# A hybrid decoder step on one core: heads rotated ahead of their inverse roots, negated maxima as biases, value chunks dealt out anew and added by DMAs

## What is computed

```python
def _layer(x, pe, pos, g_mix, w_in, g_v, w_s, b_s, g_q, g_k, w_oa, w_ob, w_o,
           g_ffn, w_ff1, w_ff2, g_ple, w_ple_gate, w_ple_proj, mix_a, mix_b):
    z = _rmsnorm(x, g_mix) @ w_in
    u, va, q, k, v, gate_a, gate_b = jnp.split(z, cuts, axis=-1)
    u = jax.nn.gelu(u)
    va = _rmsnorm(jax.nn.gelu(va), g_v)
    a = mix_a(u, va, w_s, b_s)
    q = _rotary(_rmsnorm(q.reshape(*lead, N_HEADS_B, HEAD_DIM), g_q), pos)
    k = _rotary(_rmsnorm(k.reshape(*lead, N_HEADS_B, HEAD_DIM), g_k), pos)
    b, kv_states = mix_b(q, k, v)
    merged = jax.nn.sigmoid(gate_a) * (a @ w_oa) + jax.nn.sigmoid(gate_b) * (b @ w_ob)
    x = x + merged @ w_o
    x = x + jnp.square(jax.nn.relu(_rmsnorm(x, g_ffn) @ w_ff1)) @ w_ff2
    gate = jax.nn.sigmoid(_rmsnorm(x, g_ple) @ w_ple_gate)
    x = x + gate * (pe @ w_ple_proj)
```

## Time and profile before

| | us |
|---|---|
| median of three runs | 1136.82 (1135.38 to 1138.96) |
| the profiled execution | 1137.38 |
| its span in the trace | 1136.0 |
| busy in it: PE, DVE, ACT, POOL | 1060.5, 719.9, 430.3, 229.7 |

### The profile page before, as it was taken

How to read it: one execution, slowest core, us unless ns; L and a number is a source line. 1 busy time by engine, 2 the same in 40 slices (tenths; PEclk the granted TensorE clock), 3 DMA queues, 4 the chain that set the end, 5 groups by cost and what they waited for, 6 DMA issues and landing times.

```text
span 1136.0 us, 21037 instructions
## 1 busy us (share of the span) xinstructions
PE 1060.5 (93%) x8448; PEld 1043.8 (92%) x8448; DVE 719.9 (63%) x995; ACT 430.3 (38%) x737; POOL 229.7 (20%) x367
## 2 busy tenths in 40 slices
PE   5989889998998989897999999999999999999996
PEld 5989879898888989887999999999999999999996
DVE  5669988888789866998947335443444444444552
ACT  5242355445533645424236443411421332233331
POOL 2331112102230001369800111100101101002300
PEclk9999989999999889899899999999999999999999
DMA  6645736676467743458763224564564555554412
GB/s 189 205 131 196 229 124 193 196 230 205 151 228 250 208 141 121 124 172 222 221 217 113 88 92 158 175 203 167 193 198 160 197 190 172 192 189 158 168 64 79
DMA packets 131007, 196.17 MB, mean 173 GB/s; under 512 B 31984, under 2 KB 108240, under 8 KB 129136
## 3 DMA queue, kind: packets, MB, share of 16 engines
q1 hardware_dynamic: 106448, 123.54, 34.0%
q0 software_dynamic: 10112, 63.08, 17.1%
q10 hardware_dynamic: 14368, 8.46, 2.5%
HBM read 186.07 MB, written 62.00 MB: 218 GB/s over the span
## 4 chain that ended last, share of the span: by engine, by line
PE 54%; DVE 23%; POOL 8%; issue 6%; ACT 4%; DMA 3%; SPq 1%; ACTq 0%; DVEq 0%; POOLq 0%
PE gm L1046 48%; POOL kv L1797 6%; DVE w_lo L1315 4%; DVE kv L1436 3%; DVE kv L1477 2%; DVE fin L1356 2%; DVE sq L1335 2%; ACT w_hi L617 2%; DVE acc L1483 2%; POOL st L1767 1%; DVE st L1327 1%; SPq L508 1%; DMA out_kvp<-fin 1%; PE gm L1022 1%; DVE rot L1365 1%
## 5 line engine op out<-in xcount | busy, mean ns | idle before, releaser
L1046 PE MATMUL gm<-h_hi,w_hi 128*128 128x272 f32 x1088 | 231.0, 294 | 11.2 <-DVE z L1379 4.9
L1046 PE MATMUL gm<-h_hi,w_lo 128*128 128x272 f32 x1088 | 227.8, 291 | 0.0
L1046 PE MATMUL gm<-h_lo,w_hi 128*128 128x272 f32 x1088 | 226.9, 290 | 0.0
L1315 DVE TENSOR_TENSOR w_lo<-w_raw,w_hi 128x1024 fp32r<-128x1024 f32 x150 | 178.0, 1227 | 75.2 <-ACT w_hi L617 73.4
L617 ACT CAST w_hi<-w_raw 128x1024 fp32r<-128x1024 f32 x150 | 150.1, 1047 | 152.1 <-PE gm L1046 116.5
L1022 PE MATMUL gm<-w_hi,h_hi 128*128 128x256 f32 x640 | 190.0, 297 | 4.4 <-DVE w_lo L1315 2.3
L1046 PEld LDWEIGHTS gm<-h_hi,w_hi 128*128 128x128 f32 x1088 | 173.1, 191 | 13.0 <-issue 11.1
L1023 PE MATMUL gm<-w_hi,h_lo 128*128 128x256 f32 x640 | 183.8, 287 | 0.0
L1024 PE MATMUL gm<-w_lo,h_hi 128*128 128x256 f32 x640 | 182.9, 286 | 0.0
L1046 PEld LDWEIGHTS gm<-h_lo,w_hi 128*128 128x128 f32 x1088 | 173.4, 191 | 0.0
L1046 PEld LDWEIGHTS gm<-h_hi,w_lo 128*128 128x128 f32 x1088 | 172.5, 192 | 0.0
(11 more groups left out here) (254 smaller groups left out, 1463.4 us busy)
## 6 DMA issues: line engine op xcount, KB each, us to landing
w_raw<-in_w_ff SPq DMA_DIRECT2D x64, 512.0 KB, 5.2
out_kvs<-in_cache_kv_w POOLq DMA_DIRECT2D x64, 510.0 KB, 4.2
w_raw<-in_w_in SPq DMA_DIRECT2D x60, 512.0 KB, 5.5
kv<-in_cache_kv_w SPq DMA_DIRECT2D x128, 128.0 KB
kv<-in_cache_kv_w SPq DMA_DIRECT2D x64, 256.0 KB
out_kvs<-in_cache_kv_w POOLq DMA_DIRECT2D x32, 508.0 KB, 4.7
kv<-in_cache_kv_w POOLq DMA_DIRECT2D x128, 64.0 KB, 3.5
w_raw<-in_w_o SPq DMA_DIRECT2D x8, 512.0 KB, 4.8
```

What stands on the lines that cost most here:

```text
L1046: last = nc.tensor.matmul(gm[:, 2 * b2 + half, 0:HALF], w, x[:, k0 + k, half * HALF:(half + 1) * HALF], start=first, stop=end)
L1315: vec.tensor_tensor(w_lo[:, r, cols], w_raw[:, hh], w_hi[:, r, cols].bitcast(F32), ALU.subtract).then_inc(w_lo_done, 1)
```

## The change

1. **Chunks.** `CHUNKS_AT` is given by a string, one digit a slot. Group 0's keys now start in slot 11 (before 9), its values run in slots 26 to 38 (before 24 to 37), with 11 of them in slots 30 to 35. Group 1's values run in slots 54 to 71 (before 72), 16 of 17 by slot 64. Group 2 has its keys in 72 to 79, its values in 80 to 84.
2. **Adds by DMA.** A value chunk of groups 0 and 1 after the first is only multiplied by DVE; POOL then issues a DMA that adds `kv` to `acc` (`add_values`, `accum_op=ALU.add`), in the slot after, once the add before it has landed. Who reuses the ring place or reads `acc` waits for `values_added` (`wait_values`).
3. **Heads.** DVE applies gain and rotation to the unscaled `z` in the unit's own slot (`rotate_heads`) and scales by the inverse root last (`scale_heads`), for sub 0 and 1 in the same slot behind the maxima, for sub 2 in the next. The two half products of the rotation become one. The factor 1/8 is put into the q gain by POOL once.
4. **Maxima.** `tensor_reduce` writes the negated maximum, which is ACT's bias; `ngm` goes. Both pieces of a pair are taken in its even slot, by DVE and by ACT.
5. **ACT's order.** Squares of sample rows, the tanh of gelu and the exponentials of the chunk weights move to the start of the next slot. DMAs of v sample rows go from ACT to POOL. The factor of gelu moves into the square, and DVE's two instructions for its inner part become one.
6. **Head of the program.** `gx_b` is issued ahead of `ident`; PE runs 22 matmuls on `ones` before its first transposes and 8 behind them.

```diff
+CHUNKS_IN_SLOT = ("000000000002203112002102012102212213002103003002112111"
+                  "103113122110000001131100121213200000000000")
+CHUNKS_AT = {_s: int(_n) for _s, _n in enumerate(CHUNKS_IN_SLOT)}
...
-        if s in S_AT:
+        if s in S_AT and not (paired(S_AT[s]) and S_AT[s] % 2):
             jobs.append(("piece", S_AT[s]))
+            if paired(S_AT[s]):
+                jobs.append(("piece", S_AT[s] + 1))
...
+        def added_by_dma(n):
+
+            return CHUNKS[n][0] == "values" and CHUNKS[n][1] < 2 and n != CH_FIRST["values", 0]
...
+        def wait_values(engine, n):
+
+            if added_by_dma(n):
+                engine.wait_ge(values_added, 16 * added_count(n))
+            else:
+                engine.wait_ge(values_used, sum(c[0] == "values" and not added_by_dma(x) for x, c in enumerate(CHUNKS[:n + 1])))
...
@@ ACT @@
-                    nc.scalar.activation(sq[0:NS, r, 0:256], z[0:NS, r, 0:256], ACT.Square).then_inc(sq_ready, 1)
...
+                if s >= 1 and UNITS[s - 1][4] == 2 and UNITS[s - 1][1] in ("k", "q", "va"):
+                    square_samples(s - 1)
+                if s >= 1 and UNITS[s - 1][1] in ("va", "u"):
+                    gelu_tanh_of(s - 1)
...
-                        e = nc.scalar.activation(prob[:, j % 2, w * x:w * x + w], s_bank(j)[:, w * x:w * x + w], ACT.Exp, scale=SCALE,
-                                                 bias=ngm[:, j % 2, x:x + 1])
+                        e = nc.scalar.activation(prob[:, j % 2, w * x:w * x + w], s_bank(j)[:, w * x:w * x + w], ACT.Exp,
+                                                 bias=O[:, x if g_ else 2 * pair + x, hd, 65:66])
...
@@ PE @@
+            pe.wait_ge(zeroed, 1)
+            busy(22)
             pe.wait_ge(ident_in, 16)
             x_transposes(0)
             x_transposes(1)
+            busy(8)
...
@@ DVE, rotate_heads @@
                     if fin_count(n - 2):
                         dve.wait_ge(fin_stored[n % 2], fin_count(n - 2))
...
+                vec.tensor_tensor(f.rearrange("p (h d) -> p h d", d=HD), z[0:rows, r, 0:256 * nt].rearrange("p (h d) -> p h d", d=HD),
+                                  bc(gain, 1, 4 * nt), ALU.mult).then_inc(z_used, 1)
...
+            def scale_heads(u):
+                rows, nt = shape_kq(u)
+                n = kqn(u)
+                dve.wait_ge(rstd_ready, n + 1)
+                f = fin[0:rows, n % 2, 0:256 * nt].rearrange("p (h d) -> p h d", d=HD)
+                vec.tensor_tensor(f, f, bc(st[0:rows, 1, 16 + 8 * (n % 2):16 + 8 * (n % 2) + 4 * nt], 2, HD), ALU.mult).then_inc(fin_ready, 1)
...
-                link(vec.tensor_reduce(m, sv, AX.X, ALU.max))
-                vec.tensor_scalar(ngm[:, j % 2, 0:512 // w], m, -SCALE, None, ALU.mult).then_inc(max_ready, 1)
+                vec.tensor_reduce(m, sv, AX.X, ALU.max, negate=True).then_inc(max_ready, 1)
...
                 if first:
                     out.then_inc(values_used, 1)
+                elif added_by_dma(n):
+                    out.then_inc(values_scaled, 1)
...
@@ POOL @@
+            gp.tensor_scalar(gq_b[:], gq_b[:], SCALE, None, ALU.mult).then_inc(gain_scaled, 1)
...
+            def add_values(n):
+
+                nk = CHUNKS[n][3]
+                pool.wait_ge(values_scaled, added_count(n))
+                if added_count(n) > 1:
+                    pool.wait_ge(values_added, 16 * (added_count(n) - 1))
+                else:
+                    pool.wait_ge(values_used, 1)
+                pool.dma_start(acc[:, 0:nk], kv[:, n % RING, 0:nk], accum_op=ALU.add).then_inc(values_added, 16)
...
+                for n in CH_AT.get(s - 1, []):
+                    if added_by_dma(n):
+                        add_values(n)
```

More of the change, by code:

```diff
@@ L652, in evacuate @@
                     r = stage_slot(u)
-                    nc.scalar.activation(two(sq[:, r]), src, ACT.Square).then_inc(sq_ready, 1)
+                    nc.scalar.activation(two(sq[:, r]), src, ACT.Square, scale=GELU_A ** 0.5).then_inc(sq_ready, 1)
                     nc.scalar.copy(two(z[:, r]), src).then_inc(unit_out, 1)
@@ L704, in evacuate, with gelu_tanh_of, square_samples @@
                     square_x(m, m, zc(u))
+            def gelu_tanh_of(u):
+                _, kind, _, _, sub = UNITS[u]
+                act.wait_ge(gelu_arg, GELU.index(u) + 1)
+                r = (zc(u) - 1) % 2
+                rows, n = (128, NT) if kind == "u" else (128, 512) if sub < 2 else (NS, 256)
+                nc.scalar.activation(sq[0:rows, r, 0:n], sq[0:rows, r, 0:n], ACT.Tanh, scale=GELU_B).then_inc(gelu_tanh, 1)
+            def square_samples(u):
+                r = (zc(u) - 1) % 2
+                act.wait_ge(unit_out, u + 1)
+                nc.scalar.activation(sq[0:NS, r, 0:256], z[0:NS, r, 0:256], ACT.Square,
+                                     scale=GELU_A ** 0.5 if UNITS[u][1] == "va" else 1.0).then_inc(sq_ready, 1)
             def merged_hi(m):
@@ L837, in tile_hi @@
                                    x_bank(a, half).rearrange("p (k n) -> p k n", k=4)).then_inc(h_hi_done, 1)
+            act.dma_start(gx_b[:], t["g_mix"].partition_broadcast(128)).then_inc(gx_in, 16)
             act.dma_start(ident[:], t["c_ident"]).then_inc(ident_in, 16)
[L840 removed]
             square_tile(0)
@@ L918, in _ @@
                     act.wait_ge(al_arg, 1)
-                    nc.scalar.activation(al[:], al[:], ACT.Exp, scale=SCALE).then_inc(al_exp, 1)
+                    nc.scalar.activation(al[:], al[:], ACT.Exp).then_inc(al_exp, 1)
                 if s == 65:
@@ L1251, in y_transposes, with busy @@
                 nc.tensor.transpose(psO[0:NS, 0:128], xT[:, m, SEQ:NT], ident[:]).then_inc(t_ready, 1)
+            def busy(n):
+                for _ in range(n):
+                    nc.tensor.matmul(gm[:, 3, 0:128], ones[:], ones[:], start=True, stop=True)
+            pe.wait_ge(zeroed, 1)
+            busy(22)
             pe.wait_ge(ident_in, 16)
@@ L1388, in gelu_inner @@
                 dve.wait_ge(sq_ready, sq_count(u))
-                link(vec.tensor_scalar(sq[0:rows, r, 0:n], sq[0:rows, r, 0:n], GELU_A, 1.0, ALU.mult, ALU.add))
                 dve.wait_ge(unit_out, u + 1)
-                vec.tensor_tensor(sq[0:rows, r, 0:n], sq[0:rows, r, 0:n], z[0:rows, r, 0:n], ALU.mult).then_inc(gelu_arg, 1)
+                vec.scalar_tensor_tensor(out=sq[0:rows, r, 0:n], in0=sq[0:rows, r, 0:n], scalar=1.0, in1=z[0:rows, r, 0:n],
+                                         op0=ALU.add, op1=ALU.mult).then_inc(gelu_arg, 1)
             def gelu_outer(u):
@@ L1649, in _ @@
                 if kind in ("k", "q"):
-                    sum_squares(s)
-                if kind in ("va", "u"):
+                    if sub < 2:
+                        sum_squares(s)
+                    rotate_heads(s)
+                if kind == "u" or kind == "va" and sub < 2:
                     gelu_inner(s)
@@ L1695, in _ @@
                     take_scores(job)
+                if kind in ("k", "q") and sub < 2:
+                    scale_heads(s)
                 for g_ in range(NG):
@@ L1824, in _ @@
                 p, kind, g, i, sub = UNITS[s]
+                if s >= 1 and UNITS[s - 1][1] == "v" and UNITS[s - 1][4] == 2:
+                    _, _, vg, vi, _ = UNITS[s - 1]
+                    pool.wait_ge(unit_out, s)
+                    cols = slice(256 * vi, 256 * vi + 256)
+                    pool.dma_start(t[f"kvs{vg}"][:, 1, WIN[vg] - T:WIN[vg], cols],
+                                   vn[NS * vg:NS * vg + NS, cols]).then_inc(vn_stored[vg], 16)
                 if kind in ("k", "q"):
```

119 lines of the change are left out of this document (55 added, 64 removed).

## The result

| | before | after |
|---|---|---|
| median, us | 1137.82 (4 runs) | 1231.53 (1227.55 to 1236.01, 4 runs) |
| ratio | | 1.0827 (95%: 1.0800 to 1.0853) |
| the profiled execution, its span | 1137.38, 1136.0 | 1236.01, 1234.6 |

The forecast was 1100 us in a range from 1082 to 1138. The change is 94 us slower, beyond the rival that was given 1176.

The account below looks back on a forecast made before the run. PE, busy 1060.5 of 1136.0 us, was taken as the bound, to gain only by less waiting or a higher clock. Recovered 50 less 6 (stores) and 7 (adds) made 37; 1137.4 - 37 - 0.6 = 1100 us, range 1082 to 1138.

Parts of the forecast that it names:

- I take 5 with the issue: Value chunks of groups 0 and 1: one 512 KB DMA add takes 5 us including its issue.
- priced at 7 us: Cost of the DMA adds: 4 us in group 1's v units plus 3 us from 349 us on.
- The bounds of 3 and 11: Limits for one add: below 3 us (2.0 and a second 256 KB), above 11 us (5.5 twice).
- Rival 1: DMA adds become the bound at 9 us each, giving 1176 us; decides from 7.6 us an add; chance 0.12.
- Heads rotated first: Rotating in the unit's own slot makes `fin` earlier; PE's 9.8 us and DVE's 14.7 us of waits go.
- a gain of most of 25 us: q, k and v units, 26 to 349 us: three quarters of 33.0 us of idle and clock loss recovered.
- DVE's 14.7 us for inverse roots: DVE's waits for GpSimd's inverse roots, 14.7 us, were to go with heads rotated first.
- The 17: 349 to 446 us (value rows, gated inputs, scores of group 2): four fifths of 21.1 us recovered.
- The merge: 446 to 547 us (merge of branch A and of the attention): a quarter of 21.7 us recovered, 5 us.
- The stores, 6 us: DVE overwriting `fin` waits for k-unit stores: 12 k units at 0.5 us each, 6 us lost.
- rival 2: DVE waits 2 us per k unit for stores, or adds take about 6 us; 1118 us; chance 0.24.
- The head: Head of the program: added matmuls raise PE's clock for unit 0, 3 us won; they take 5.3 us of idle time.

Follow-up runs that it names:

- e1: The changed kernel with all value chunks added by VectorE again instead of by DMA; 1139.83 us, 1.0028 of the kernel before.
- e12: e11 with the chunk table of e8, which keeps chunks out of the slots of sample rows; 1106.79 us, 0.9713 of the kernel before.
- e2: e1 with the chunk table (`CHUNKS_AT`) of the kernel before; 1142.07 us, 1.0038 of the kernel before.
- e11: e1 with gain, rotation and scaling of a unit in the next slot, as in the kernel before; 1113.40 us, 0.9773 of the kernel before.
- e5: e1 with a pair's two maxima ahead of the gain product and rotation in q and k slots; 1134.52 us, 0.9968 of the kernel before.
- e8: e5 with a chunk table that keeps chunks out of the sample rows' slots from slot 24 to 53; 1121.20 us, 0.9842 of the kernel before.
- e10: The change with its 33 DMA adds as plain copies, so value chunks are not summed; 1194.26 us, 1.0488 of the kernel before.

## Why the prediction was wrong, point by point

**The price of an add, "I take 5 with the issue", is the step that failed most.** From start to start it is 8.0 us (220 to 268 us) and 8.6 (512 to 547 us, four adds), and 7.4 to landing; the adds by DMA, priced at 7 us, cost 92 against adds on VectorE. The value was taken "nearest to GpSimd's own copy" at 4.2, a row from DRAM to DRAM that waits for no other. An add on an idle chip does take 4.8. Loads and a cache copy beside it bring the landing from 4.5 to 6.2 us; the rest, up to 7.4, is not explained by any run. The Trainium skill (DMA: Bandwidth & Descriptors, Anatomy of one DMA) gives an estimate of 3.2 us for 512 KB: a copy alone lands in 2.8, an add alone in 4.5 and one in the layer in 7.4, so the trace does not agree for adds. The bounds of 3 and 11 held it, and they should have set the range: by the prediction's own rule the sign turns at 7.6.

**Rival 1 was the mechanism, and too cheap.** Its rule gives 1176 at 9 us; at 8 to 8.6 us the kernel took 1231. It hid 40 us in the ring and in slots without chunks, and priced no clock: in units 36 to 53 PE's own work took 12 us more than in e1 (117.0 against 105.2). Which part of the 92 us comes through the ring, through the late inverse roots and through the panels is not separated. The signs named for it (GpSimd over 100 us in its own DMAs, scaling behind GpSimd, chunks behind loads) are all in the list. Against it stood only the copy's row.

**"Heads rotated first" was taken for a gain of most of 25 us; in the unit's own slot rotation and scaling lose 26 against the next slot.** The prediction counted what `fin` wins by being early (PE's wait for it did fall, from 9.8 to 2.2 us in e1), not what stands behind the rotation. DVE's 14.7 us for inverse roots were to go with it; in e1 they are 27.1, because the scaling now follows in the same slot. The sentence on the stores named the queue (the join, both maxima, the chunks), but for the wait, not for the 1.6 us of work itself. By stretch, in us won (e1, and e12 with neither adds nor early slot, against the earlier trace rows):

| units | forecast won | e1 | e12 |
|---|---|---|---|
| head | 3 | 2.1 | 1.4 |
| 1 to 53, q, k, v | 25 | -15.1 | 18.2 |
| 54 to 64 | 17 | 4.4 | 3.6 |
| 65 to 80, the merge | 5 | 13.2 | 13.2 |
| 81 to 111 (before from 547.1 to 684.4 us) | 0 | -4.2 | -5.9 |

Ahead of unit 81 36 of the 50 us were reachable, by another order and another table than the change's. The 17 was too much; the stretch of `va` and of the scores of group 2, which are not paired, gives 4, and no run takes its waits apart. The merge was too little; e2, with the old table, wins 5.8 there, so the table makes 7.4 of the 13.2. Behind unit 80 the prediction expected nothing either way, and 5.9 us are lost in e12, all but 0.1 in units 81 to 95 (77.5 us wide against 71.7): the clock is 0.96 there in place of 1.00, and PE waits 2.9 us for `sm`, which it did not before. No run shows the cause.

**The stores, 6 us,** are of the right order: DVE waits 11.2 us for those of k heads in the change, but in 4 places and not in 12, and 5.7 us in 3 places for sample rows of q on their way to `q_rows`, which the prediction did not count. What this costs PE no run isolates, nor rival 2.

**Chunks.** That the table is a term of its own was missed. The slots of sample rows, whose units keep PE busy for 1.8 to 6.1 us in e1, now hold up to three key chunks, 7.2 us of DVE's work. Corrected, it gives 6.6 us (e11 to e12) and 13 (e5 to e8).

**The head.** The size was right by the traces: unit 0 ends at 23.9 us in place of 26.6, which is 2.7 for the 3. Its cover was thinner than thought: the matmuls on `ones` take 8.0 us, not 5.3, and end 0.1 us before the first transposes.

```profile
1.84 7.96 PE L1287 MATMUL gm<-ones 128*128 128x128 f32 x44 [1.84 <-POOL V L1819]
9.89 1.06 PE L1130 MATMUL psT<-ident,xn 128*128 128x128 f32 x8
```

**The range.** Its lower end is said to be 55 us won, with 3 for the adds, 3.5 at the head and nothing for stores. These terms give 50 + 0.5 - 3 = 47.5, an end at 1089 and not at 1082. It changes nothing here.

## What to carry to other kernels

A chain of DMAs in which each waits for the one before is an engine: price it from issue to issue under the load that stands beside it, times its length, before work is moved to it; here 1.3 us of VectorE was exchanged for 8 us of a queue. When an operation moves to an earlier place in an in-order program, count not only what it gains but what stood behind that place and is now late by its length. When a change of several parts lands far off, take its largest part out first: here it showed at once that there were two causes, and in the end that the rest, in another order, wins 2.9% (e12).

## What the runs showed of the hardware

- A DMA that accumulates SBUF into SBUF lands in 4.5 us for 512 KB where a copy takes 2.8, both alone, and GpSimd spends 0.86 us to issue it where the copy takes 0.53. In the packets of its queue the 33 adds appear with one write's bytes (80.06 MB against 63.08 before, 17 MB more), while the queue's busy share rose from 17.1% of 1136 us to 23.9% of 1235: 101 us of all 16 DMA engines, 3.1 us an add. The 33 plain copies of e10 brought it from 17.0% of 1136 (e1) to 20.5% of 1195: 52 us, 1.6 a copy.
- Copies of 512 KB from GpSimd's and from ScalarE's queue land alike when alone, 2.8 and 2.9 us.
- Beside loads the copy loses more than the add: 2.0 us against 1.2. The DMA engines' busy share does not tell how long an add takes: 5.7 us at 1.03 with weight loads alone beside it, 7.4 in the layer, where the share was 0.78 at most in the stretches with adds.
- A stall is paid twice. Where PE waited most (units 36 to 53) its granted clock was 0.80, a mean between the levels of 1.2 and 2.4 GHz, and the same matmuls took 17% longer than at 1.00.
